# Sliding-window scores of two query heads: from zero-padded keys to two 64-row tiles of the array

## Chip, cores and metric

One core of a Trainium2 chip runs the kernel. The metric is the device time of one execution in microseconds (us); the median of three runs before the change is 1658.73 us.

## The reference, cut to what matters

One layer of a decoder is computed for a prompt of 512 tokens and for 8 samples of 4 tokens. A combined projection feeds two branches, a gated DeltaNet with 8 heads and a sliding-window attention; their sum goes through an output projection and a mixture of 64 experts. The change touches the attention over the prompt:

```
s = einsum('bnqkgd,bnskd->bnkgqs', q, k) * 64 ** -0.5     # 4 blocks of 128 queries, 256 keys each
s = where(valid, s + bias, -inf)                         # T5 bias by head and distance
m = max(max(s, -1), sink)
p = exp(s - m);  p = p / (sum(p, -1) + exp(sink - m))
o = einsum('bnkgqs,bnskd->bnqkgd', p, v)
```

There are 16 query heads of 64 channels and 2 KV heads; eight query heads share a KV head. A block of 128 queries sees its own 128 keys and the 128 before them; the first block sees its own alone.

## The kernel before, in words

The order of work is written out by hand: each engine has its own instruction list, and counting semaphores tie them. After a start-up part (norm of the input, rows of K and V, gates), every engine runs a loop over h = 0..7. Turn h computes DeltaNet head h and the two query heads 2h and 2h+1, which lie in one group of 128 channels: the channels of the first of them (u = 0) on partitions 0 to 63 of `sqT`, those of the second (u = 1) on 64 to 127. After the loop come the samples' attention, the output projection, routing and the experts.

Within a turn TensorE first projects (L1121 to L1128, then the rows of L1146 in four portions with other products between them), then builds the triangular inverses of the four 128-row chunks by repeated squaring: `square(k)` and `grow(k)` (both through the helper at L1152), six levels. ScalarE and VectorE copy each level out of PSUM (L875, L1685, L1689). The attention's four blocks n = 0..3 are laced between these levels: `scores(n)` (L1230), the softmax on VectorE (`softmax(n)`, L1701 to L1706: add the bias, maximum, maximum with the sink, negate, sink minus maximum), the exponentials on ScalarE (`probs(n)`, L882), transposes (`turn_p(n)`, L1245), a copy of them (`ptc(n)`, L891), and the product with V (`pv(n)`, L1258). Small 32-row products for the samples (L1269, L1281, L1288, L1296) stand ahead of each `scores(n)` on TensorE's queue; each waits for VectorE (`s_smp_done`). The recurrence over the chunks (L1328 to L1346) ends the turn.

`kz` holds the keys four times over: `kz[:, u, kv, :]` has the keys of KV head kv on the 64 partitions of half u and zeros on the other half. So `scores(n)` multiplies all 128 rows of `sqT` with `kz[:, u, kv]`, once for each u, and the zeros leave the other query head out. Its address depends on h through `ds(kv)`. Both results lie in one PSUM bank, bank 7 for even n, bank 5 for odd n, and one addition of VectorE over both adds the bias. GpSimd clears `kz` at the start (L630).

GpSimd's part of a turn is `gm` (L671) and a small product (L673) for the decays, two masks of the exponentials (L676, L678), the output gates and the state's stores.

Of the kernel before, what the change touches and what calls it, by code (L numbers as in the profile page):

```python
# [8 lines left out]
ALU = mybir.AluOpType  # L9
ACT = mybir.ActivationFunctionType  # L10
AX = mybir.AxisListType
P = 128
# [5 lines left out]
class Chain:  # L18
# [12 lines left out]
    def step(self, ins):  # L31
        self.inc(ins)
        self.eng.wait_ge(self.sem, self.value())
# [9 lines left out]
def ds(i, n=1):  # L43
    return bass.ds(i, n)
# [6 lines left out]
def program(nc, x_prompt, x_sample, conv_state, dn_state, cache_k, cache_v, w_in, conv_w, a_log, dt_bias, dn_norm_w,  # L51
# [4 lines left out]
    TP, TS = x_prompt.shape[0], x_sample.shape[0]  # L56
    NP = TP // P
    NT = NP + 1
# [5 lines left out]
    HD = 64  # L64
# [20 lines left out]
    with ExitStack() as ctx:  # L85
# [6 lines left out]
        PB = [ctx.enter_context(nc.psum_tensor(f"PB{i}", [P, 512], F32)) for i in range(8)]  # L92
# [14 lines left out]
        sc = sb("sc", [P, 256])  # L107
# [4 lines left out]
        def cut(*shape, parts=P):  # L112
            n = 1
            for s in shape:
                n *= s
            a = arena[0:parts, top[0]:top[0] + n]
            top[0] += n
            assert top[0] <= 37632, top[0]
            if len(shape) == 2:
                return a.rearrange("p (a b) -> p a b", a=shape[0])  # L120
            if len(shape) == 3:
                return a.rearrange("p (a b c) -> p a b c", a=shape[0], b=shape[1])
            if len(shape) == 4:
                return a.rearrange("p (a b c d) -> p a b c d", a=shape[0], b=shape[1], c=shape[2])
            return a
# [1 line left out]

        hT = cut(KC, T)
        nmix = cut(KC)
        kz = cut(2, 2, TP)  # L130
        skd = cut(2, TS)
        kvrow = cut(NT, 4 * HD)
        qz = cut(B, 2, 2, 16)
# [51 lines left out]
        Vm = sb("Vm", [TS, B, P])  # L185
        wqT = sb("wqT", [P, B, 2, L])
        wqo = sb("wqo", [P, 2, TS])
        xh = kz.rearrange("p a b c -> p (a b c)")
        biasS = sb("biasS", [P, 2, 133])
        mixer_end = top[0]  # L190

# [424 lines left out]
        def _(pool):  # L616
# [9 lines left out]
            for t in (ones[:, :], m_le[:, :], m_gt[:, :], m_ge[:, :], blk[:, :, :], bsel[:, :]):  # L626
                ch.inc(pool.memset(t, 1.0))
            ch.inc(pool.memset(ident[:, :], 0.0))
            for t in (rawP[:, :, 0:3], kz, qz.rearrange("p b v u k -> p (b v u k)"), scal, sc[:, 80:160]):
                ch.inc(pool.memset(t, 0.0))  # L630
            pool.memset(eps_t[:, 0:1], EPS).then_inc(s_setup0, 1)
            pool.memset(eps_t[:, 1:2], -0.5 * 4.852030263919617).then_inc(s_setup0, 1)
# [36 lines left out]
            with pool.Fori(0, H) as h:  # L669
                pool.wait_ge(s_hs_ready, h * 2 + 1)  # L670
                pool.tensor_tensor(gm, m_le[:, :].unsqueeze(1).to_broadcast([P, NP, P]),  # L671
                                   hsc[:, 0, 0:NP].unsqueeze(2).to_broadcast([P, NP, P]), ALU.mult).then_inc(s_gm_ready, 1)
                pool.tensor_scalar(sS[:, 8, 0:TS], s_le[:, :], hsc[0:TS, 0, NP:NT], None, ALU.mult).then_inc(s_gm_ready, 1)  # L673

                pool.wait_ge(s_E_exp, h + 1)
                pool.tensor_tensor(Es, E, m_gt[:, :].unsqueeze(1).to_broadcast([P, NP, P]), ALU.mult).then_inc(s_Em_ready, 1)  # L676
                pool.wait_ge(s_Em_ready, h * 2 + 1)
                pool.tensor_tensor(E, E, m_ge[:, :].unsqueeze(1).to_broadcast([P, NP, P]), ALU.mult).then_inc(s_Em_ready, 1)  # L678

                for i, n in enumerate(gate_rows):  # L680
                    R = rows_of[n]
                    pool.wait_ge(s_rows_done, 1 + h * NT + (i + 1))
                    pool.tensor_tensor(gates[0:R, n, 0, :], gates[0:R, n, 0, :], gates[0:R, n, 1, :], ALU.mult).then_inc(s_ss_done, 1)
                    pool.wait_ge(s_ss_done, h * NT + (i + 1))
                    pool.tensor_tensor(gates[0:R, n, 0, :], gates[0:R, n, 0, :], dnw[0:R, :], ALU.mult).then_inc(s_gate_done, 1)
                    if i == 2:
                        pool.wait_ge(s_crow_ready, h + 1)
                        pool.sem_inc(s_pool_passed, 1)
                        pool.dma_start(p_conv[:, :, ds(h * P, P)], crow[0:3, :, :]).then_inc(s_conv_out, 16)
                        pool.dma_start(s_conv[:, :, ds(h * P, P)], crow[3:27, :, :]).then_inc(s_conv_out, 16)  # L690
                pool.wait_ge(s_smp_ps, h * 11 + 8)
                pool.tensor_tensor(Sb[:, :, :], Sb[:, :, :], hgl.unsqueeze(2).to_broadcast([P, B, P]), ALU.mult).then_inc(s_decay_done, 1)
                pool.wait_ge(s_sW_done, h * 3 + 3)
                pool.tensor_tensor(Vm[:, :, :], sS[:, 6, :].unsqueeze(1).to_broadcast([TS, B, P]),
                                   bsel[:, :].unsqueeze(2).to_broadcast([TS, B, P]), ALU.mult).then_inc(s_Vm_done, 1)
                pool.wait_ge(s_S_done, h * NP + NP)
                pool.sem_inc(s_pool_passed, 1)
                pool.dma_start(p_dn[ds(h), :, :].rearrange("a k v -> (a k) v"), St).then_inc(s_pdn_out, 16)
                pool.wait_ge(s_sS_done, 1 + h + 1)
                pool.sem_inc(s_pool_passed, 1)  # L700
                pool.dma_start(s_dn.rearrange("b h k v -> h k b v")[ds(h), :, :, :].rearrange("a k b v -> (a k) b v"), Sb[:, :, :]).then_inc(s_sdn_out, 16)

                pool.wait_ge(s_conv_out, h * 32 + 32)
                pool.wait_ge(s_pdn_out, h * 16 + 16)
                pool.wait_ge(s_sdn_out, h * 16 + 16)
                pool.sem_inc(s_stored, 1)
# [62 lines left out]
        def _(act):  # L769
# [26 lines left out]
            act.activation(g8(2), g8(2), ACT.Ln).then_inc(s_g_ready, 1)  # L796
            act.wait_ge(s_kd_ps, 1)
            for v in range(2):
                act.activation(kz[v * HD:(v + 1) * HD, v, v, :], PB[4][v * HD:(v + 1) * HD, :], ACT.Copy).then_inc(s_kd_done, 1)
                act.activation(skd[v * HD:(v + 1) * HD, v, :], PB[5][v * HD:(v + 1) * HD, 0:TS], ACT.Copy).then_inc(s_kd_done, 1)  # L800
            act.wait_ge(s_ba_ready, 6)
            gs = tmp[:, 280:424]
# [251 lines left out]
        def _(pe):  # L1054
# [51 lines left out]
            with pe.Fori(0, H) as h:  # L1106
# [48 lines left out]
                qT = qk[:, 0, 0:TP].rearrange("p (n k) -> p n k", n=NP)  # L1155
                kT = qk[:, 1, 0:TP].rearrange("p (n k) -> p n k", n=NP)
                rows(0)
                pe.wait_ge(s_gm_ready, h * 2 + 2)
                pe.wait_ge(s_cst_ready, h + 1)
                for n in range(NP):  # L1160
                    last = mm(PB[7][:, n * P:(n + 1) * P], gm[:, n, :], m_gt[:, :], start=True, stop=True)
# [58 lines left out]
                def scores(n):  # L1220
                    lo = P if n == 0 else 0
                    if n == 0:
                        pe.wait_ge(s_Et_done, h + 1)
                    elif n == 1:
                        pe.wait_ge(s_rows_done, 1 + h * NT + 4)
                    else:
                        pe.wait_ge(s_sc_add, h * NP + (n - 1))
                    bank = PB[7 if n % 2 == 0 else 5]
                    for u in range(2):
                        last = mm(bank[:, u * 256 + lo:(u + 1) * 256], sqT[:, n * P:(n + 1) * P],  # L1230
                                  kz[:, u, ds(kv), (n - 1) * P + lo:(n + 1) * P].rearrange("p a k -> p (a k)"), start=True, stop=True)
                    last.then_inc(s_sc_ps, 1)

                def turn_p(n):
# [29 lines left out]
                pe.wait_ge(s_rows_done, 1 + h * NT + NT)  # L1264
                tr(b6[0:TS, 224:352], ks_, ident[:, :])
                tr(b6[0:TS, 352:480], co[:, 2, TP:T], ident[:, :]).then_inc(s_smp_ps, 1)
                pe.wait_ge(s_gm_ready, h * 2 + 2)
                pe.sem_inc(s_pe_passed, 1)
                mm(b6[0:TS, 0:TS], sS[:, 8, 0:TS], s_gt[:, :], start=True, stop=True).then_inc(s_smp_ps, 1)  # L1269
                scores(0)  # L1270
# [264 lines left out]
        def _(dve):  # L1535
# [62 lines left out]
            dve.wait_ge(s_kd_ps, 1)  # L1598
            for q in range(2):
                lo, hi = slice(32 * q, 32 * q + 32), slice(HD + 32 * q, HD + 32 * q + 32)  # L1600
                cp(kz[hi, 1, 0, :], PB[4][lo, :]).then_inc(s_kd_done, 1)
                cp(kz[lo, 0, 1, :], PB[4][hi, :]).then_inc(s_kd_done, 1)
                cp(skd[hi, 0, :], PB[5][lo, 0:TS]).then_inc(s_kd_done, 1)
                cp(skd[lo, 1, :], PB[5][hi, 0:TS]).then_inc(s_kd_done, 1)
            dve.wait_ge(s_slots_moved, 16)
            KD = 92
            with dve.Fori(0, H) as h:
                ch.loop(h, KD)

# [81 lines left out]
                def softmax(n):  # L1691
                    lo = P if n == 0 else 0
                    a = att[:, n % 2, :]
                    bank = PB[7 if n % 2 == 0 else 5]
                    if n >= 2:
                        dve.wait_ge(s_pt_ps, h * NP + (n - 1))
                        dve.wait_ge(s_p_exp, h * 3 * NP + 3 * (n - 1))
                    dve.wait_ge(s_sc_ps, h * NP + (n + 1))
                    dve.wait_ge(s_bias_in, 16)
                    snk = sinkb[:, ds(h * 2, 2)]  # L1700
                    step(tt(sm[:, n % 2, :, lo:], bank[:, :].rearrange("p (u k) -> p u k", u=2)[:, :, lo:],  # L1701
                            bias[:, ds(h * 2, 2), lo:], ALU.add))
                    step(dve.tensor_reduce(a[:, 0:2], sm[:, n % 2, :, lo:], AX.X, ALU.max))
                    step(tt(a[:, 0:2], a[:, 0:2], snk, ALU.max))
                    step(ts(a[:, 2:4], a[:, 0:2], -1.0, None, ALU.mult))
                    tt(a[:, 4:6], snk, a[:, 0:2], ALU.subtract).then_inc(s_sc_add, 1)  # L1706
# [401 lines left out]
```

## Time and profile before

| what | us |
|---|---|
| median of 3 runs | 1658.73 (1657.37 to 1659.74) |
| the profiled execution | 1663.34 |
| its span, first to last instruction | 1661.6 |
| TensorE matmul busy | 1418.0 (85%) |
| VectorE busy | 827.4 (50%) |
| ScalarE busy | 333.9 (20%) |
| GpSimd busy | 235.0 (14%) |
| L1230 (scores), TensorE busy, 128 matmul instructions | 32.8 |

PE is TensorE's matmul and PEld its weight load, DVE is VectorE, ACT ScalarE, POOL GpSimd, SP the engine that issues most DMAs; a q behind a name is the sequencer, which waits and issues. A row of the timeline reads: start, length in us, engine, line, operation, written tile, read tiles, shapes, count, and in brackets the idle time before it and what ended that. Ends of matmuls are modelled, so the modelled lengths of consecutive matmuls overlap. The granted clock is a share of TensorE's 2.4 GHz.

### The profile page before, as it was taken

Reading aid. Unit: us, or ns where it says so; the run is one execution under the profiler, and the core shown is the slowest. Engines: PE = TensorE matmul, PEld = TensorE weight load, DVE = VectorE, ACT = ScalarE, POOL = GpSimd, SP = SyncE. Lnnn points to the kernel's source line nnn. Section 1 sums busy time; section 2 is a strip of 40 time slices with the busy share of each in tenths; the row PEclk is TensorE's granted clock in tenths of the full one; section 3 lists DMA queues with packets and bytes.
Section 4 is the critical chain, followed back from the end, with each engine's and each line's share of the span. In section 5 each row is a group of like instructions: output and inputs, shape, how many; then the busy total and the mean of one; then the engine's idle time right before and its main releaser. Section 6 shows DMA issues by size and latency. Waiting matters only on the chain.

```text
span 1661.6 us, 20978 instructions
## 1 busy us (share of the span) xinstructions
PE 1418.0 (85%) x6824; PEld 811.9 (49%) x6824; DVE 827.4 (50%) x1742; ACT 333.9 (20%) x901; POOL 235.0 (14%) x356
## 2 busy tenths in 40 slices
PE   5799999999999999999999878866887878888791
PEld 4557558466485575765846754532332323233230
DVE  1386476774865857748667522462322323222225
ACT  3122123122221231222212311100111101111112
POOL 2210111021101210111012100013111111111100
PEclk9899799998998999989999879867998989899895
DMA  8821020130210302102101240169999999999985
GB/s 190 152 53 39 27 68 23 38 79 27 53 38 27 90 2 71 45 27 53 38 27 39 115 162 40 47 242 291 420 411 415 403 413 398 403 387 417 401 331 187
DMA packets 126880, 277.79 MB, mean 167 GB/s; under 512 B 21500, under 2 KB 95158, under 8 KB 102134
## 3 DMA queue, kind: packets, MB, share of 16 engines
q1 hardware_dynamic: 103990, 196.21, 33.3%
q10 hardware_dynamic: 10704, 66.06, 11.0%
q0 software_dynamic: 12160, 15.19, 2.9%
q8 instruction: 13, 0.21, 0.1%
q14 instruction: 13, 0.11, 0.0%
HBM read 272.43 MB, written 30.62 MB: 182 GB/s over the span
## 4 chain that ended last, share of the span: by engine, by line
PE 65%; DMA 21%; DVE 7%; ACT 4%; issue 2%; SPq 0%; ACTq 0%; DVEq 0%; POOLq 0%; POOL 0%
DMA arena<-in_w_up 16%; PE PB L1128 13%; PE PB L1146 10%; PE PB L1482 9%; PE PB L1152 7%; PE PB L1406 4%; DMA arena<-in_w_gate 3%; PE PB L1230 2%; PE PB L1123 2%; PE PB L1258 2%; DVE arena L1628 1%; PE PB L1121 1%; PE PB L1346 1%; PE PB L1337 1%; PE PB L1085 1%
## 5 line engine op out<-in xcount | busy, mean ns | idle before, releaser
L1482 PE MATMUL PB<-arena 128*64 128x512 f32 x1024 | 268.9, 674 | 87.2 <-DMA arena<-in_w_up 71.6
L1128 PE MATMUL PB<-arena 128*128 128x512 f32 x512 | 224.0, 595 | 0.0
L1482 PEld LDWEIGHTS PB<-arena 128*64 128x64 f32 x1024 | 77.6, 154 | 250.5 <-issue 153.4
L2000 DVE TENSOR_SCALAR arena<-arena 128x256 f32<-128x256 f32 x32 | 9.5, 296 | 340.4 <-ACT arena L993 340.2
L1152 PE MATMUL PB<-arena 128*128 128x128 f32 x1280 | 167.6, 286 | 6.2 <-ACT arena L871 5.5
L1146 PE MATMUL PB<-arena 128*128 128x384 f32 x512 | 170.8, 487 | 0.0
L1152 PEld LDWEIGHTS PB<-arena 128*128 128x128 f32 x1280 | 156.8, 199 | 14.9 <-ACT arena L871 7.4
L1128 PEld LDWEIGHTS PB<-arena 128*128 128x128 f32 x512 | 96.0, 190 | 118.6 <-issue 118.1
L932 ACT ACTIVATE arena<-PB 128x512 f32<-128x512 f32 (+3 forms) x116 | 59.9, 520 | 396.4 <-PE PB L1490 224.3
L1502 PE MATMUL PB<-arena 128*64 128x512 f32 x512 | 118.6, 605 | 11.1 <-issue 9.6
L1146 PEld LDWEIGHTS PB<-arena 128*128 128x128 f32 x512 | 95.4, 190 | 63.2 <-issue 3.8
L1628 DVE RECIPROCAL arena<-sig 128x384 f32<-128x384 f32 (+1 forms) x40 | 102.0, 2550 | 1.4
L1656 DVE RECIPROCAL arena<-arena 128x544 f32<-128x544 f32 x24 | 85.3, 3554 | 0.8
L1502 PEld LDWEIGHTS PB<-arena 128*64 128x64 f32 x512 | 35.5, 138 | 71.0 <-issue 66.1
L1406 PE MATMUL PB<-arena 128*128 128x512 f32 x128 | 58.7, 620 | 0.4 <-DVE arena L1833 0.4
L722 POOL COPY gidx<-gidx 128x1 int32 (+1 forms) x32 | 5.9, 184 | 366.1 <-PE PB L1472 258.6
L2002 DVE RECIPROCAL arena<-arena 128x256 f32<-128x256 f32 x32 | 56.1, 1753 | 1.1
L676 POOL TENSOR_TENSOR arena<-arena,m_gt 128x512 f32<-128x512 f32 x8 | 12.4, 1555 | 291.9 <-ACT arena L855 291.9
L1123 PE MATMUL PB<-arena 128*32 128x256 f32 x128 | 51.0, 586 | 0.0
L1124 PE MATMUL PB<-arena 128*32 128x256 f32 x128 | 51.0, 586 | 0.0
L875 ACT ACTIVATE arena<-PB 128x512 f32<-128x512 f32 x48 | 28.7, 597 | 107.5 <-PE PB L1152 107.5
L1689 DVE TENSOR_TENSOR arena<-PB,arena 128x512 f32<-128x512 f32 x48 | 33.0, 688 | 33.6 <-PE PB L1152 32.7
(433 smaller groups left out, 2025.6 us busy)
## 6 DMA issues: line engine op xcount, KB each, us to landing
arena<-in_w_gate SPq DMA_DIRECT2D x64, 1024.0 KB, 11.5
arena<-in_w_down SPq DMA_DIRECT2D x64, 1024.0 KB, 19.0
arena<-in_w_up ACTq DMA_DIRECT2D x60, 1024.0 KB, 14.8
arena<-in_w_in SPq DMA_DIRECT2D x58, 512.0 KB, 6.2
Sb<-in_state_dn SPq DMA_DIRECT2D x8, 512.0 KB, 4.0
out<-Sb POOLq DMA_DIRECT2D x8, 512.0 KB, 3.9
arena<-in_w_out SPq DMA_DIRECT2D x1, 4096.0 KB, 12.3
arena<-in_w_up SPq DMA_DIRECT2D x4, 1024.0 KB, 9.2
```

The source lines that it names most:

```text
L932: cpa = lambda o, i, **k: act.activation(o, i, ACT.Copy, **k)
L1123: mm(PB[6][64:96, 0:256], xs, wch[:, c, 0:4:2, :], start=first, stop=end)
L1124: last = mm(PB[6][96:128, 0:256], xs, wch[:, c, 1:4:2, :], start=first, stop=end)
L1128: last = mm(PB[g][:, :], wch[:, c, g, :], hT[:, c, 0:TP], start=c == 0, stop=c == KC - 1)
L1146: last = mm(gate_bank[(n + 1) % 2][0:R, 0:3 * P], hT[:, c, n * P:n * P + R], wrow[:, c, :, :].rearrange("p g k -> p (g k)"), start=c == 0, ...
L1152: last = mm(PB[bank][:, n * P:(n + 1) * P], lhs[:, n, :], rhs[:, n, :], start=start, stop=stop)
L1406: last = mm(PB[2 * (n % 2) + q][:, :], hT[:, c, n * P:(n + 1) * P], wo[:, c, q * 512:(q + 1) * 512], start=c == 0, stop=c == KC - 1)
L1482: last = mm(gu_bank[a][half[k], :], xT[:, a, c, half[k]], wgu[a][:, k, :, c, :], start=c == 0, stop=c == KC - 1)
L1502: last = mm(PB[4 + q][half[k], :], hidT[:, a, c, half[k]], wdn[a][:, k, c, q * 512:(q + 1) * 512], start=c == 0, stop=c == FE // P - 1)
L1628: step(dve.reciprocal(gates[0:R, n, :, :], s))
L1656: step(dve.reciprocal(ex[:, g, :], ex[:, g, :]))
L2002: dve.reciprocal(hb[:, a, :], hb[:, a, :]).then_inc(s_hid_own, 1)
```

## The change

The keys of a KV head are stored once for each half of the partitions, in `kz[:, kv, :]`, with no zeros between. At the start of each turn GpSimd copies the half of `kz` that belongs to this turn's KV head into `kcur`, so that TensorE reads a fixed address. `scores(n)` multiplies rows 0 to 63 of `sqT` with rows 0 to 63 of `kcur`, and rows 64 to 127 with rows 64 to 127: two tiles of 64 rows of the array. Their results go to two banks, 5 for u = 0 and 7 for u = 1, in the left or right half by the parity of n. Since both blocks now share the banks, every block's scores wait for the softmax of the block before (`s_sc_add`). VectorE adds the bias in two instructions, one for each bank. GpSimd no longer clears `kz`.

```
-        kz = cut(2, 2, TP)
+        kz = cut(2, TP)
+        kcur = cut(TP)
...
-            for t in (rawP[:, :, 0:3], kz, qz.rearrange("p b v u k -> p (b v u k)"), scal, sc[:, 80:160]):
+            for t in (rawP[:, :, 0:3], qz.rearrange("p b v u k -> p (b v u k)"), scal, sc[:, 80:160]):
...
                 pool.tensor_scalar(sS[:, 8, 0:TS], s_le[:, :], hsc[0:TS, 0, NP:NT], None, ALU.mult).then_inc(s_gm_ready, 1)
+                pool.wait_ge(s_o_done, 1 + h * NT)
+                pool.tensor_copy(kcur, kz[:, ds(h // 4), :].rearrange("p a k -> p (a k)")).then_inc(s_gm_ready, 1)
...
                     if n == 0:
                         pe.wait_ge(s_Et_done, h + 1)
-                    elif n == 1:
                         pe.wait_ge(s_rows_done, 1 + h * NT + 4)
+                        pe.wait_ge(s_gm_ready, h * 3 + 3)
                     else:
-                        pe.wait_ge(s_sc_add, h * NP + (n - 1))
-                    bank = PB[7 if n % 2 == 0 else 5]
+                        pe.wait_ge(s_sc_add, h * NP + n)
+                    pe.sem_inc(s_pe_passed, 1)
                     for u in range(2):
-                        last = mm(bank[:, u * 256 + lo:(u + 1) * 256], sqT[:, n * P:(n + 1) * P],
-                                  kz[:, u, ds(kv), (n - 1) * P + lo:(n + 1) * P].rearrange("p a k -> p (a k)"), start=True, stop=True)
+                        half = slice(u * HD, (u + 1) * HD)
+                        last = mm(PB[5 + 2 * u][:, (n % 2) * 256 + lo:(n % 2 + 1) * 256], sqT[half, n * P:(n + 1) * P],
+                                  kcur[half, (n - 1) * P + lo:(n + 1) * P], start=True, stop=True)
                     last.then_inc(s_sc_ps, 1)
...
-                    step(tt(sm[:, n % 2, :, lo:], bank[:, :].rearrange("p (u k) -> p u k", u=2)[:, :, lo:],
-                            bias[:, ds(h * 2, 2), lo:], ALU.add))
+                    for u in range(2):
+                        ch.inc(tt(sm[:, n % 2, u, lo:], PB[5 + 2 * u][:, (n % 2) * 256 + lo:(n % 2 + 1) * 256],
+                                  bias[:, ds(h * 2 + u), lo:].rearrange("p a k -> p (a k)"), ALU.add))
+                    dve.wait_ge(s_dve_own, ch.value())
```

## Rows read from the trace of the kernel before

**Rows 1.** The page, the chain that ended last, shares by engine
```profile
PE 65%; DMA 21%; DVE 7%; ACT 4%; issue 2%; SPq 0%; ACTq 0%; DVEq 0%; POOLq 0%; POOL 0%
```

**Rows 2.** The chain in order of time: start, us, what; first projections of three heads
```profile
76.30 7.06 PE PB L1128 x16
...
191.45 7.06 PE PB L1128 x16
...
300.65 7.06 PE PB L1128 x16
```

**Rows 3.** The chain in order of time, scores in the fourth head, blocks 0 and 2
```profile
471.40 0.64 PE PB L1230 x4
...
480.00 1.12 PE PB L1230 x4
```

**Rows 4.** Timeline, TensorE, block 2 of the fourth head and what follows
```profile
480.00 1.13 PE L1230 MATMUL PB<-arena 128*128 x4
...
480.96 0.55 PE L1258 MATMUL PB<-arena,pT 128*128 x4
```

**Rows 5.** One line, L1230: ns min/median/max; matmuls of block 2, sequencer in all heads
```profile
L1230 PE MATMUL PB<-arena x4: 379/379/479, 480.0 to 480.7; 128*128 x4
...
L1230 PEldq FUSED_REGOPS  x48: 46/51/128, 137.4 to 919.8; - x48
```

**Rows 6.** Timeline, TensorE, start of the fourth head, four 32-column tiles
```profile
403.36 0.53 PE L1121 MATMUL PB<-arena 128*32 128x192 f32 x1
...
403.38 0.64 PE L1124 MATMUL PB<-arena 128*32 128x256 f32 x1
...
403.68 0.53 PE L1121 MATMUL PB<-arena 128*32 128x192 f32 x1
```

**Rows 7.** Timeline, TensorE, a 64-row stage between two whole-array ones
```profile
416.85 0.34 PE L1135 MATMUL PB<-ident,srow 64*128 64x64 f32 x2
...
417.12 0.70 PE L1128 MATMUL PB<-arena 128*128 128x512 f32 x1
```

**Rows 8.** Timeline, VectorE around block 0, and TensorE's load of L1281
```profile
471.30 0.68 DVE L1685 COPY arena<-PB 128x512 f32<-128x512 f32 x1
...
471.90 0.33 DVE L1718 TENSOR_SCALAR sS<-PB,hbeta 32x128 f32<-32x128 f32 x1
...
472.88 0.40 DVE L1701 TENSOR_TENSOR sm<-PB,arena 128x256 f32<-128x256 f32 x1
...
475.35 0.18 DVE L1730 TENSOR_TENSOR sS<-PB,sS 32x32 f32<-32x32 f32 x1
...
475.64 0.09 PEld L1281 LDWEIGHTS PB<-ident,sS 32*32 32x32 f32 x1 [0.22 <-issue]
```

**Rows 9.** Groups by line and shape: count, busy us, mean ns, idle before
```profile
L2004 DVE TENSOR_TENSOR arena<-arena,PB 128x256 f32<-128x256 f32 x32 | 13.5, 420 | 1.1
...
L1629 DVE TENSOR_TENSOR arena<-arena,PB 128x128 f32<-128x128 f32 x32 | 9.2, 287 | 1.1
```

**Rows 10.** Timeline, VectorE in blocks 1 and 2, scores of block 3
```profile
477.08 0.69 DVE L1701 TENSOR_TENSOR sm<-PB,arena 128x512 f32<-128x512 f32 x1 [0.74 <-PE PB L1230]
...
483.00 0.16 DVE L1706 TENSOR_TENSOR att<-arena,att 128x2 f32<-128x2 f32 x1
...
484.74 1.13 PE L1230 MATMUL PB<-arena 128*128 x4
```

**Rows 11.** Timeline, GpSimd and ScalarE at the start, GpSimd in the fourth head
```profile
2.97 2.54 POOL L630 MEMSET arena<- 128x9 f32 x4
...
10.46 1.06 ACT L779 ACTIVATE arena<-mixed 128x1024 f32<-128x1024 f32 x1 [8.27 <-DMA arena<-in_norm_mix_w]
...
407.82 1.04 POOL L671 TENSOR_TENSOR arena<-m_le,arena 128x512 f32<-128x512 f32 x1 [3.41 <-DMA out<-Sb]
```

**Rows 12.** Stretches: busy us of PE, PEld, DVE, ACT, POOL; granted clock; DMA share, GB/s
```profile
163.40:190.70 27.30, 25.30 (x127) 17.50 (x127) 10.78 (x39) 4.44 (x21) 6.41 (x6) 0.50 0.09 25
...
497.90:501.30 3.40, 3.40 (x16) 2.75 (x14) 2.10 (x9) 0.15 (x1) 0.82 (x1) 0.50 0.00 0
501.30:511.60 10.30, 8.21 (x42) 5.26 (x40) 4.64 (x15) 4.04 (x20) 2.51 (x2) 1.00 0.02 6
```

More of the change, by code:

```diff
@@ L187, in program @@
         wqo = sb("wqo", [P, 2, TS])
-        xh = kz.rearrange("p a b c -> p (a b c)")
         biasS = sb("biasS", [P, 2, 133])
@@ L798, in _ @@
             for v in range(2):
-                act.activation(kz[v * HD:(v + 1) * HD, v, v, :], PB[4][v * HD:(v + 1) * HD, :], ACT.Copy).then_inc(s_kd_done, 1)
+                act.activation(kz[v * HD:(v + 1) * HD, v, :], PB[4][v * HD:(v + 1) * HD, :], ACT.Copy).then_inc(s_kd_done, 1)
                 act.activation(skd[v * HD:(v + 1) * HD, v, :], PB[5][v * HD:(v + 1) * HD, 0:TS], ACT.Copy).then_inc(s_kd_done, 1)
@@ L1157, in _ @@
                 rows(0)
-                pe.wait_ge(s_gm_ready, h * 2 + 2)
+                pe.wait_ge(s_gm_ready, h * 3 + 2)
                 pe.wait_ge(s_cst_ready, h + 1)
@@ L1266, in _ @@
                 tr(b6[0:TS, 352:480], co[:, 2, TP:T], ident[:, :]).then_inc(s_smp_ps, 1)
-                pe.wait_ge(s_gm_ready, h * 2 + 2)
+                pe.wait_ge(s_gm_ready, h * 3 + 2)
                 pe.sem_inc(s_pe_passed, 1)
@@ L1600, in _ @@
                 lo, hi = slice(32 * q, 32 * q + 32), slice(HD + 32 * q, HD + 32 * q + 32)
-                cp(kz[hi, 1, 0, :], PB[4][lo, :]).then_inc(s_kd_done, 1)
-                cp(kz[lo, 0, 1, :], PB[4][hi, :]).then_inc(s_kd_done, 1)
+                cp(kz[hi, 0, :], PB[4][lo, :]).then_inc(s_kd_done, 1)
+                cp(kz[lo, 1, :], PB[4][hi, :]).then_inc(s_kd_done, 1)
                 cp(skd[hi, 0, :], PB[5][lo, 0:TS]).then_inc(s_kd_done, 1)
@@ L1605, in _ @@
             dve.wait_ge(s_slots_moved, 16)
-            KD = 92
+            KD = 96
             with dve.Fori(0, H) as h:
@@ L1693, in softmax @@
                     a = att[:, n % 2, :]
-                    bank = PB[7 if n % 2 == 0 else 5]
                     if n >= 2:
```

## The prediction

> **What bounds the kernel now.** I began with the chain of waits by engine: TensorE holds 65% of it, DMA 21%, VectorE 7% [rows 1]. In its list in order of time the first projection of a head (L1128) shows how long a head lasts: 115.15 us for the first (76.30 to 191.45) and 109.20 for the second (191.45 to 300.65); the six later ones repeat that closely [rows 2]. So some 880 of the 1661.6 us are eight heads, bound by TensorE; the rest, mostly experts whose weights arrive by DMA, the change does not touch. Inside a head the same list has the four score blocks of L1230 on the chain: 0.64 us for block 0 and 1.12 for block 2, which stands for three alike [rows 3].
>
> The timeline then says what block 2 consists of: four matmul instructions (two query heads, each in two passes), the first at 480.00, and the next line's first at 480.96, so a block takes 0.96 [rows 4]. Its first matmul lasts 479 ns against 379 for the others [rows 5]: a weight load of 0.10 that nothing hides, as a 32-row stage stands ahead. So a pass takes (0.96 - 0.10)/4 = 0.215.
>
> **The change part by part.** *Scores as two 64-row tiles.* The trace has no pair of row tiles that work at once. The nearest rows are the four 32-column tiles of L1121 to L1124: their first passes start within 0.02 us of each other (403.36 to 403.38), the second pass of L1121 only at 403.68 [rows 6]. Four different tiles ran at once, pass by pass. For two row tiles I take the same: 2 x 0.215 = 0.43 of streaming in place of 0.86. The other end is no overlap at all, 0.86.
>
> What comes after a block gets dearer. Now L1230 and what follows use the whole array. After the change a 64-row stage stands between, and the trace has one: the two 64-row transposes of L1135 between two runs of L1128. They start at 416.85 and their modelled end is 417.19; the next whole-array matmul starts at 417.12, thus 0.07 before that end [rows 7]. For a score pass, whose modelled end lies 0.379 after its start, that is a gap of 0.379 - 0.07 - 0.215 = 0.09 after the last pass; and then the first load of the new stage is exposed, 0.10 as in rows 5. The way in costs what it costs now, since a 32-row stage (L1269, L1281, L1288, L1296) stands ahead of each block already. New block: 0.10 + 0.43 + 0.09 + 0.10 = 0.72, against 0.96: 0.24 saved. Without any overlap it is 1.15, 0.19 lost.
>
> A rule of the Trainium skill speaks against the change here: "TensorEngine Tiling (Array Packing)", Tiling Modes, Key Properties, says that a change of tiling mode, other than a change of tile, drains TensorE. Rows 7 agree, with the 0.09 above. With the rule the sum is the one below; without it each block would save 0.43 and the total would come to 9.1 us.
>
> *Block 0 gains nothing.* The squaring that follows it needs VectorE's copy of L1685, which runs from 471.30 to 471.98; the block itself lies between 471.40 and 472.04 on the chain [rows 3, 8]. A shorter block waits for that copy.
>
> *The split bias addition on VectorE (L1701).* One instruction over both heads becomes two, since they lie in two banks. For blocks 1 to 3, 128x512 at 0.69 becomes two of 128x256; L2004, of that form and out of PSUM, lasts 0.420. For block 0, 0.40 becomes two of 128x128, and L1629 of that form lasts 0.287 [rows 8 to 10]. Instructions in a row overlap (L1718 starts 0.08 before L1685 ends [rows 8]), so I get 2 x 0.42 - 0.08 - 0.69 = +0.07 and 2 x 0.287 - 0.08 - 0.40 = +0.09, and take 0.10 for block 0, with a register instruction more. In block 0 this is on the path: the VectorE rows from L1685 at 471.30 to L1730 at 475.35 show no idle time, and PE's L1281 waited for L1730 (it ends at 475.53, the load comes at 475.64 after 0.22 idle) [rows 8]. So 0.10 is lost per head; bounds 0, were the pair as fast as the one, and 0.17 with no overlap. In blocks 1 to 3 VectorE waits for the scores before L1701, 0.74 us in block 1 [rows 10]; it gets them some 0.3 earlier, which covers 0.07. If that cover went, 0.21 per head.
>
> *Semaphores.* Scores of block n now wait for the softmax of block n-1, in every block. Ahead of blocks 1 and 2 stands a matmul that waits for a later VectorE instruction anyway. Block 3 is the new one: the last step it waits for ends at 483.16, the block starts at 484.74 [rows 10], so there is 1.6 us of slack; behind the wait on TensorE's queue stand the products with V, the transposes and the next squaring, for which ScalarE and VectorE wait. The added semaphore instruction ahead of each block is priced by the register instruction that vanishes (48 of them, median 51 ns [rows 5]): nothing for blocks 2 and 3, 0.05 for block 1, whose wait now stands alone ahead of the load; bounds 0 and 4 x 0.05.
>
> *Copy of the keys on GpSimd.* 128x512 per head. The product L671 of that size lasts 1.04 and starts at 407.82 [rows 11]; the copy stands behind it and ahead of the wait for the exponentials, some 60 us before scores are due (471.40). The wait for the head before is over by then, since GpSimd has just waited for that head's state stores. Bounds 0 and 8 x 1.04; I take nothing. *Clearing of kz.* At the start it falls away, up to 2.54 us of GpSimd; but ScalarE's first work waits for the input's DMA until 10.46 [rows 11], later than all of that. Nothing.
>
> **Sum.** Per head 3 x 0.24 - 0.10 - 0.05 = 0.57; times eight, 4.6 us. The ends: all overlap and no drain or extra cost, 3 x 0.43 = 1.29 per head, 10.3; no overlap with 0.17 and 0.20 lost, -(3 x 0.19 + 0.37) = -0.94 per head, 7.5 us slower. The profiled execution took 1663.34 (span 1661.6 and 1.7 around it), so it would take 1658.7; the median of the runs is 1658.73, 4.6 under that execution, and the same subtraction gives 1654.1, which I forecast.
>
> **Rivals.** *1. The two tiles do not run side by side (slower).* For it: no row shows two row tiles at once. Against: rows 6 show four column tiles doing so. Price: 3 x 0.19 + 0.15 = 0.72 per head, 5.8 us, 1664.5. It decides once the streaming of a block exceeds 0.62 (0.43 plus the 0.19 that drain and load take back).
>
> *2. Half an overlap; the change does only half of what it says.* If the second head's first pass begins only when the first head's second pass has begun, three passes stand in a row: 0.10 + 0.645 + 0.19 = 0.94, about as now. With 0.15 lost against 3 x 0.02 the change costs 0.1 per head, 1659.4: no change. The interleaved starts of rows 6 speak against it. The Trainium skill, "TensorE: Matmul & The Clock Gate", Part 3, says that matmuls start strictly in program order, and by that rule one head's two passes would come ahead of the other's; rows 6 do not look like that.
>
> *3. The clock after a head.* In the first head TensorE's clock is at 1.2 GHz (granted 0.50) from 163.40 to 190.70. In a later head it falls too, but 497.90 to 501.30 is low and then it is back at 2.4 GHz (1.00 until 511.60) [rows 12]. To that I put down the 5.95 us between the first head and the others. Heads last as long as this pattern takes to repeat, so each later head meets it at the same point of its work. With heads 0.57 shorter the point wanders, and which kind a head becomes may change in either direction. If the first head recovers early too: 4.6 + 5.95 = 10.5, 1648.2. If one more head stays low: 1.4 slower, 1660.1, no change; two more, 7.3 slower, 1666.0. The rows show both kinds and don't say where one turns into the other.
>
> *4. Gain on paper only.* The scores come earlier, but ScalarE's probabilities or VectorE bind the next step. Blocks 1 to 3 have TensorE on the chain, so I see at most half lost: 1656.4.
>
> **How the numbers follow.** A difference of 0.2% (3.3 us) is about what can be told from no change. Chances: forecast 0.36 (its own range 1652 to 1657; 0.29 faster, 0.07 within); early recovery 0.15; one head more at the low clock 0.09; two or more 0.15; no overlap 0.10; half 0.09; gain on paper 0.06 (0.02 faster). Faster 0.46, same 0.29, slower 0.25. The range runs from 1645, past the early recovery, to 1666, where two more low heads end; left out are more than two such heads, the far end of no overlap, and several early ones.
>
> **What would show it.** Right: L1230's matmuls of the two heads start within 0.02 us of each other; from a block's first matmul to the next line's first 0.72 instead of 0.96 in blocks 1 to 3; the load after it exposed; block 0 no shorter on the chain and L1281 0.1 later; heads of 108.6. The forecast is wrong if passes start one behind the other, if a block still takes 0.9 or more, or if heads differ from each other by some 6 us, which would be the clock.

## The result and the profile after

The changed kernel takes 1646.94 us (median of 6 runs, 1640.67 to 1649.11) against 1659.24 for the kernel before on the same chip (1657.24 to 1667.30): 12.3 us faster, ratio 0.9904 with a 95% interval of 0.9875 to 0.9933. The forecast was 4.6 us. The profiled execution took 1647.58 (span 1645.9), 15.8 under that of before.

First the page's line on the chain of waits by engine, against [rows 1]:

```profile
PE 64%; DMA 22%; DVE 7%; ACT 4%; issue 2%; SPq 1%; ACTq 0%; DVEq 0%; POOLq 0%; POOL 0%
```

Then the chain in order of time, the first projections of all eight heads (L1130, the L1128 of before), against [rows 2]:

```profile
77.43 7.06 PE PB L1130 x16
...
186.78 7.06 PE PB L1130 x16
...
293.86 7.06 PE PB L1130 x16
...
402.00 7.06 PE PB L1130 x16
...
509.08 7.06 PE PB L1130 x16
...
614.74 7.07 PE PB L1130 x16
...
722.87 7.07 PE PB L1130 x16
...
831.63 7.06 PE PB L1130 x16
```

The bound is the same. But heads are no longer alike: 109.35, 107.08, 108.14 and 107.08 us for the first four, then 105.66, 108.13 and 108.76. The seven together take 831.63 - 77.43 = 754.2, where before they took 115.15 + 6 x 109.20 = 770.4. So 16.2 us came out of seven heads: 5.8 out of the first and 10.4 out of the six behind it. The first head starts 1.1 later than before, at the end of a weight transfer ahead of the loop; the traces below begin theirs between 75.98 and 77.39 with no pattern by kernel.

Next the timeline of TensorE in the fourth head, against [rows 4, 5]: first of the stretch from 468.10 to 468.14 alone, below the line of dots block 1 and block 2 with what follows each:

```profile
468.13 0.49 PE L1233 MATMUL PB<-arena 64*128 64x256 f32 x2
...
468.13 0.70 PE L1233 MATMUL PB<-arena 64*128 64x256 f32 x4
468.76 0.44 PE L1248 MATMUL PB<-ident,sm 128*128 128x128 f32 x2
...
471.99 0.70 PE L1233 MATMUL PB<-arena 64*128 64x256 f32 x4
472.75 0.65 PE L1261 MATMUL PB<-arena,pT 128*128 x4
473.24 0.60 PE L1248 MATMUL PB<-ident,sm 128*128 128x128 f32 x4
```

Within that short stretch the first passes of both heads have started. The four rows of a block last 0.70 together, where they lasted 1.13.

Then the chain around block 0, against [rows 8]:

```profile
462.92 0.60 DVE arena L1685
463.52 0.61 DVE arena L1688
464.14 0.14 issue
464.27 0.79 PE PB L1154 x5
```

VectorE's two additions of block 0, in the timeline:

```profile
465.02 0.47 DVE L1704 TENSOR_TENSOR sm<-PB,arena 128x128 f32<-128x128 f32 x2
465.53 0.42 DVE L1707 TENSOR_REDUCE att<-sm 128x2 f32<-128x256 f32 x1
```

And the stretches by granted clock: the end of the first head, which answers to [rows 12], and the fifth head from its middle on (columns as there):

```profile
165.40:175.60 10.20, 9.67 (x39) 7.79 (x37) 3.63 (x15) 1.47 (x5) 2.32 (x2) 0.50 0.01 2
175.70:182.40 6.70, 5.12 (x41) 3.12 (x44) 4.49 (x14) 2.97 (x16) 1.38 (x2) 1.00 0.03 10
182.50:185.90 3.40, 3.40 (x40) 2.34 (x34) 1.89 (x10) 0.00 (x0) 0.07 (x1) 0.50 0.53 154
571.60:575.00 3.40, 3.40 (x20) 3.17 (x19) 1.97 (x11) 1.54 (x6) 0.00 (x0) 0.50 0.00 0
575.00:614.60 39.60, 36.38 (x309) 29.84 (x307) 24.13 (x81) 12.07 (x46) 5.34 (x4) 1.00 0.05 15
```

Before, the first head was low for 27.3 us without a break; now it recovers in between. The fifth head, which was low twice for 10.2 us in all, is low once, for 3.4, and keeps the full clock to its end. That is the shortest head, 105.66.

How much of the 16.2 us is work and how much clock? Up to the last small product ahead of the products of the carried state (L1304 before, L1307 after) the second head runs at the full clock in both traces; it comes 79.97 us after the head's first projection before, 79.49 after. So the edits save 0.48 us a head by themselves, 3.4 in seven heads and 3.9 in eight. The other 12.8 would be the clock. That is an inference from two traces; the experiments test it.

### The profile page after: what moved, and what is told of

Read it like the earlier page. It is cut to its first block, busy times and chain, and to the rows that moved or that the text cites. A ratio compares the mean times of both kernels' runs of the same rounds, so it can differ in the third digit from the quotient of the medians.

```text
span 1645.9 us, 21025 instructions
## 1 busy us (share of the span) xinstructions
PE 1396.2 (85%) x6824; PEld 794.9 (48%) x6824; DVE 830.6 (50%) x1774; ACT 333.9 (20%) x901; POOL 237.8 (14%) x363
## 4 chain that ended last, share of the span: by engine, by line
PE 64%; DMA 22%; DVE 7%; ACT 4%; issue 2%; SPq 1%; ACTq 0%; DVEq 0%; POOLq 0%; POOL 0%
DMA arena<-in_w_up 17%; PE PB L1130 14%; PE PB L1148 10%; PE PB L1485 9%; PE PB L1154 7%; PE PB L1409 4%; DMA arena<-in_w_gate 3%; PE PB L1261 2%; PE PB L1125 2%; DVE arena L1631 1%; PE PB L1123 1%; PE PB L1340 1%; PE PB L1087 1%; PE PB L1174 1%; PE PB L1233 1%
## 5 line engine op out<-in xcount | busy, mean ns | idle before, releaser
L1485 PE MATMUL PB<-arena 128*64 128x512 f32 x1024 | 263.9, 663 | 84.0 <-DMA arena<-in_w_up 69.7
L1130 PE MATMUL PB<-arena 128*128 128x512 f32 x512 | 224.0, 595 | 0.0
L1130 PEld LDWEIGHTS PB<-arena 128*128 128x128 f32 x512 | 96.0, 190 | 118.6 <-issue 118.1
L1505 PE MATMUL PB<-arena 128*64 128x512 f32 x512 | 119.5, 609 | 16.2 <-issue 13.9
L1475 PEld LDWEIGHTS PB<-ident,arena 128*128 128x128 f32 x256 | 31.8, 196 | 31.0 <-issue 31.0
L1125 PE MATMUL PB<-arena 128*32 128x256 f32 x128 | 44.2, 522 | 0.0
```

What stands on the lines that cost most here:

```text
L1125: mm(PB[6][64:96, 0:256], xs, wch[:, c, 0:4:2, :], start=first, stop=end)
L1130: last = mm(PB[g][:, :], wch[:, c, g, :], hT[:, c, 0:TP], start=c == 0, stop=c == KC - 1)
L1485: last = mm(gu_bank[a][half[k], :], xT[:, a, c, half[k]], wgu[a][:, k, :, c, :], start=c == 0, stop=c == KC - 1)
L1505: last = mm(PB[4 + q][half[k], :], hidT[:, a, c, half[k]], wdn[a][:, k, c, q * 512:(q + 1) * 512], start=c == 0, stop=c == FE // P - 1)
```

## The experiments

Theory 1: the edits save some 0.5 us a head, and the rest is what the granted clock does when the work lies differently under it. Theory 2: the operations of the change are worth the whole 1.5 us a head. In the sections below "direct" is the shift of that same product (L1304 or its counterpart) at the full clock, per head; totals are ratios to the kernel before in the same session.

### Other changes of a head's length, with and without the row tiles

**b_short**, the kernel before with less work in the scores: in blocks 2 and 3 it leaves out the second query head's scores against one half of its keys.

```
-                        last = mm(bank[:, u * 256 + lo:(u + 1) * 256], ...
+                        hi = P if u == 1 and n >= 2 else 0
+                        last = mm(bank[:, u * 256 + lo:(u + 1) * 256 - hi], ...
```

> The kernel before, without row tiles, fixed keys or the split addition; in the scores of blocks 2 and 3 the second query head's matmul takes 128 of its 256 keys, so those scores are left out. Each of the two matmuls falls from some 0.43 us to 0.21, so TensorE's path in a head is 0.43 us shorter, about what the change took directly (0.48). Theory 1 (direct saving 0.5 us a head, the rest of the 12.3 us is what TensorE's granted clock does once a head is no longer 109.2 us long): the total falls by clearly more than 8 x 0.43 = 3.4 us, to 1643 to 1652 from some 1659, head lengths unequal, and the stretches at a granted clock of 0.50 move from head to head as in the changed kernel. Theory 2 (the whole 12.3 us comes from the changed operations themselves, 1.5 us a head): 1655.8, every head 108.8 us.

Ratio 0.9907 (0.9872 to 0.9941), 15 us, at a direct saving of 0.33 (79.65 against 79.98 in the first head), 2.6 us in all. Its chain:

```profile
76.55 7.06 PE PB L1128 x16
...
186.16 7.06 PE PB L1128 x16
...
292.04 7.06 PE PB L1128 x16
...
397.93 7.06 PE PB L1128 x16
```

Heads of 105.9 in place of 109.2: with no row tile, no copy of keys and no split addition, the kernel gets all that the change got. Theory 2 (1655.8, heads of 108.8) is out. The direct part was 0.1 smaller than I expected.

**a_long**, the changed kernel with its saving given back in block 3:

```
-                    for u in range(2):
+                    for u in (0, 1, 0, 1) if n == 3 else (0, 1):
```

> The changed kernel with block 3's pair of score matmuls issued twice, +0.4 us a head on TensorE's path, the result unchanged. Theory 1: the head's phase against the granted clock's falls is set anew, so the total moves by another amount than 8 x 0.43 = 3.4 us; most of the 12.3 us can be lost, 1650 to 1660. Theory 2: the row tiles and the fixed keys are all there, so 1647 + 3.4 = 1650.4, every head 0.43 us longer than in the changed kernel.

Ratio 0.9949 (0.9925 to 0.9973; 1652.26), so nearly half the gain went with 0.43 us a head. The direct saving left is 0.04 (79.92 against 79.97), 0.3 us in all, and still 8 us are gained: its first five heads alternate between 108.6 and 106.5. The two theories' ranges both held this; but a kernel whose work is less by 0.04 us a head and that is 8 us faster cannot owe that to its work.

**b_long** and **b_long2**, the kernel before with the second query head's scores issued twice in block 3, and in blocks 2 and 3:

```
-                    for u in range(2):
+                    for u in (0, 1, 1) if n == 3 else (0, 1):     # b_long; n >= 2 in b_long2
```

> The kernel before with the second query head's score matmul of block 3 issued twice, +0.43 us a head on TensorE's path, the result unchanged. Theory 1 (direct part plus whatever the granted clock's pattern does at the new head length): the total does not follow the added 3.4 us; heads come out unequal or locked to another pattern, anywhere from 1650 to 1668, and a total at or below that of the kernel before would show that shortening is not what brought the extra gain. Rival (the time follows the work, 8 x 0.43 us): 1660 + 3.4 = 1663.8, every head 109.64 us with the same three low stretches.

> The same in blocks 2 and 3, +0.86 us a head. Theory 1: again not on a line with the added work (6.9 us); 1652 to 1672. Rival: 1667.2, every head 110.07 us.

Ratios 1.0065 (1.0037 to 1.0092), 11 us, and 1.0194 (1.0161 to 1.0227), 32 us, for direct costs of 0.43 and 0.87 a head, 3.5 and 6.9 us in all. My hope that a longer head might do as well as a shorter one failed: more work cost more, three and nearly five times over. Both kernels took longer than theory 1 allowed (1670.41 against at most 1668, 1691.18 against at most 1672), and longer than the rival's 1663.8 and 1667.2. So the time does not follow the added work alone, as theory 1 says, but I had sized the clock's part too small here too. In b_long2 what only the first head had before [rows 12] befalls three heads in a row. The stretch that is low in the second head:

```profile
274.30:301.40 27.10, 25.10 (x125) 17.30 (x126) 10.73 (x38) 4.43 (x21) 6.31 (x6) 0.50 0.08 23
```

And on its chain the first projections of the fourth and fifth head:

```profile
418.22 7.06 PE PB L1128 x16
...
534.24 7.06 PE PB L1128 x16
```

116.0 us for the fourth head, 6.8 more than before; the second and third take as long.

### The same pair with the clock held up

If the clock makes the difference, it must shrink to the direct part when the clock no longer falls. **b_warm** and **a_warm** are the two kernels with matmuls whose results nobody reads, put where TensorE waits; the banks they write are free by then.

```
+                def warm(bank, lo, cols, count):
+                    for _ in range(count):
+                        mm(PB[bank][:, lo:lo + cols], ident[:, :], hT[:, 0, 0:cols], start=True, stop=True)
...
                 square(1)
+                pe.wait_ge(s_Et_done, h + 1)
+                warm(7, 0, 256, 3)
                 pe.wait_ge(s_rows_done, 1 + h * NT + NT)
...
                 each(3, Rk, Tt).then_inc(s_wT_ps, 1)
+                pe.wait_ge(s_sc_add, h * NP + NP)
...
                     if n:
+                        warm(5, 0, P, 1)
                         pe.wait_ge(s_S_done, h * NP + n)
...
+                    warm(5, 0, HD if n else P, 1 if n else 3)
                     pe.wait_ge(s_vn_done, h * NP + (n + 1))
...
+                warm(0, 0, 256, 3)     # behind the last matmul of the turn
```

> The kernel before with matmuls whose results nobody reads put into TensorE's waits: three of 256 columns before the wait for the fourth gate rows, three of 128 before the first wait of the recurrence, one of 64 or 128 before each later one, three of 256 after the last matmul of a head. Theory 1: the granted clock stays at 1.00 through the loop, a head takes some 106 us instead of 109.2, total 1659 - 25 = 1634 (1628 to 1645). Theory 2: the clock may rise too, but says nothing about the change. If the extra matmuls end late, a head gets longer by up to 1 us and the total may not fall.

> The changed kernel with the same extra matmuls in the same waits. Theory 1: with the clock at 1.00 in both, this pair differs by the direct part alone, 8 x 0.48 = 3.9 us (3 to 5), so some 1630, heads of 105.5 us; the changed kernel's advantage of 12.3 us shrinks to a third. Theory 2: the pair differs by about 12 us, as without the extra matmuls.

Ratios 0.9894 (0.9866 to 0.9922) and 0.9855 (0.9820 to 0.9889). The gap between the two narrowed from 0.0096 to 0.0039, about 6 us, more than the 3.9 of theory 1; the medians (1643.99 and 1633.62) lie 10.4 apart, hardly less than the 12.3 of the plain pair. So the totals decide nothing here, and the clock was not held: it still falls some 87 us into each of the first seven heads of b_warm and five of a_warm's, whose other two take 105.0 with no low stretch. Heads with the same low time differ by about the direct part: with 3.4 us low 106.9 to 107.1 against 106.2 to 106.6, with 6.8 low 108.28 against 107.79.

What stands ahead of that fall is the same in all traces: eight products of the carried state whose moving operand has 8 columns (L1313 before, L1316 after). **b_full** and **a_full** widen it to 64 columns, of which 8 are used. The weight loads set the pace there, so it costs little. The products go to bank 5, and the later extra matmuls to bank 7:

```
-        wqT = sb("wqT", [P, B, 2, L])
+        wqT = sb("wqT", [P, 2 * B, 2, L])     # upper half cleared once
...
+                pe.wait_ge(s_sc_add, h * NP + NP)
...
-                    last = mm(b6[:, b * 2 * L:(b + 1) * 2 * L], Sb[:, b, :], wqT[:, b, :, :]...
+                    last = mm(PB[5][:, b * 64:(b + 1) * 64], Sb[:, b, :], wqT[:, b:b + 8, :, :]...
```

> b_warm with one more edit: the eight products of the carried state with 8 columns each, before the recurrence (the stretch right ahead of the last fall of the granted clock that b_warm still shows, 87 us into a head), take 64 columns each, of which 8 are used. Theory 1: the granted clock stays at 1.00 for whole heads, all of 105.6 us (105.0 for a_warm's two heads without a low stretch, plus 0.5 to 0.6), total 1636 to 1640. Theory 2 says nothing about this kernel alone.

> a_warm with the same wider products. Theory 1: heads of 105.0 us at a granted clock of 1.00, and the pair differs by the direct part alone, 0.5 to 0.6 us a head, 4 to 5 us in all: 1631 to 1635, and the scatter from run to run is smaller than in the changed kernel (1640.7 to 1649.1). Theory 2: the pair differs by 12 us. If the products of 64 columns are not hidden beside their weight loads, both heads are up to 0.5 us longer.

1632.40 (ratio 0.9845, 0.9818 to 0.9872) and 1625.66 (0.9811, 0.9783 to 0.9838). The stretch from the second head to the eighth in b_full (the clock is the third figure from the end):

```profile
182.00:815.10 633.10, 616.76 (x3350) 418.69 (x3348) 448.58 (x930) 167.78 (x486) 94.69 (x120) 1.00 0.17 46
```

The same in a_full:

```profile
181.50:811.90 630.40, 611.48 (x3350) 409.33 (x3348) 453.32 (x954) 167.65 (x486) 97.41 (x126) 1.00 0.17 46
```

The first projections of the second and the eighth head on b_full's chain:

```profile
182.08 7.06 PE PB L1128 x16
...
815.22 7.06 PE PB L1128 x16
```

And on a_full's:

```profile
181.60 7.06 PE PB L1130 x16
...
812.00 7.06 PE PB L1130 x16
```

Six heads take 633.14 and 630.40: 105.52 and 105.07 each. At one clock the change is worth 0.45 us a head, 3.6 in eight, close to the 0.48 of the first reading. Both totals lie below the expected ranges (1636 to 1640 and 1631 to 1635), and the medians differ by 6.7, where I expected 4 to 5. In the two traces the loops differ by 3.7; the other 2.3 lie behind the loop, nearly all in the experts, which are the same code in both. I did not find their cause.

This also prices the clock. In the kernel before, a later head was low twice; here is the fifth, with the stretch between:

```profile
607.10:610.50 3.40, 3.40 (x16) 2.75 (x14) 2.11 (x9) 0.16 (x1) 0.83 (x1) 0.50 0.00 0
610.50:620.80 10.30, 8.22 (x42) 5.26 (x40) 4.64 (x15) 4.03 (x20) 2.52 (x2) 1.00 0.02 6
620.80:627.60 6.80, 6.28 (x63) 4.40 (x65) 3.53 (x15) 0.24 (x1) 2.33 (x3) 0.50 0.30 86
```

Such a head took 109.20, and 105.52 at 2.4 GHz, so its 10.2 us at 1.2 GHz cost 3.7. Over seven heads the clock cost 770.4 - 7 x 105.52 = 31.8 us before and 754.2 - 7 x 105.07 = 18.7 after. Of the 16.2 us, 13.1 are clock and 3.1 work. This takes the extra matmuls and the wider products to add nothing to a head. Up to the products of the carried state they don't: these start 85.06 us into a head in the kernel before, in b_warm and in b_full alike. Behind that point no run separates them.

**b_full_long2** puts b_long2's edit into b_full, to see whether the extra matmuls multiply anything by themselves:

> b_full (extra matmuls in the waits and the wider products, clock at 1.00 through the heads) with the second query head's score matmul issued twice in blocks 2 and 3, the edit that made the kernel before 32 us slower. Theory 1 (an edit of the scores has a direct part, and the clock's falls multiply it): here only the direct part is left, about 0.43 us a block on TensorE's path where no other wait hides it: heads of 105.9 to 106.4 us in place of 105.52 and 3 to 7 us in all, 1635 to 1639. Rival (the added matmuls cost 32 us by themselves, by delaying VectorE or the recurrence): heads of 109 us, some 1660.

1640.89, ratio 0.9882 (0.9858 to 0.9906), 6 us over b_full by the ratios and 8.5 by the medians, a little above the expected 1635 to 1639. Two of its starts:

```profile
182.36 7.06 PE PB L1128 x16
...
288.75 7.06 PE PB L1128 x16
```

Heads of 106.39, 0.87 longer: with the clock held, a head grows by its added work and by nothing else. The edit that costs 32 us under a falling clock costs 6 to 8.5 under a steady one.

**a_wide** is the changed kernel with the wider products alone:

> The changed kernel with only the eight products of the carried state at 64 columns in place of 8, no extra matmuls. Theory 1: the low stretch 87.7 us into a head goes, those at 62.7 and 101 us stay in part; heads of 105 to 107 us, total 1636 to 1645. Rival (the products have nothing to do with the falls): 1647 with the same falls at 87.7 us.

1639.01, ratio 0.9877 (0.9851 to 0.9903). Its runs lie within 3.7 us of each other, those of the changed kernel within 8.4. Five of its first seven heads take 106.1, the other two 108.4; two starts on its chain:

```profile
184.85 7.06 PE PB L1130 x16
...
290.92 7.06 PE PB L1130 x16
```

As expected the fall at 87.7 us is gone from every head, and those at 63 and 101 stay in part. The products take 1.95 us in place of 1.90 (L1324 of a_full against L1316 of the changed kernel). One fall is removed by columns that hold nothing of use.

### Is it the row groups that overlap?

**a_onehalf** puts both matmuls on the same 64 rows of the array:

```
-                        half = slice(u * HD, (u + 1) * HD)
+                        half = slice(0, HD)
```

> The changed kernel with both score matmuls on partitions 0 to 63, so one row group of the array for both; the second query head's scores are left out (the first's stand in their place). If the gain of a block is the overlap of two row groups, the second matmul's passes start behind the first's, some 0.43 us later, and a block takes 1.0 to 1.1 us in place of 0.63 to 0.75, a head at equal granted clock 0.43 us a block longer for the blocks on TensorE's path. If it is the 64 rows or the two banks instead, the passes still start 7 ns apart and the block stays at 0.63 to 0.75 us. The total is one draw of the clock's pattern and tells nothing by itself.

Block 2 of its second head and what follows, in the timeline:

```profile
263.55 1.13 PE L1233 MATMUL PB<-arena 64*128 64x256 f32 x4
264.61 0.55 PE L1261 MATMUL PB<-arena,pT 128*128 x3
```

A block takes 1.06 to the next line's first matmul, 0.10 more than the whole-array block before and 0.3 more than the tiles on two row groups. So the overlap needs two row groups; 64 rows or two banks alone give nothing. Up to L1307 its second head is 0.64 us longer than before (80.61 against 79.97), and its one run took 1672.55, between b_long and b_long2, as its direct cost is. A kernel without GpSimd's copy of the keys (a_nocopy) gave no time, so no run shows what the copy and the fixed address are worth by themselves.

## Why the prediction was right in kind and wrong in size

- *Two tiles at once: right.* Both heads' first passes start within the stretch of 0.04 us shown. The tiles run pass by pass, as the column tiles of [rows 6] did. Rivals 1 and 2 are out: the second head's first pass starts ahead of the first head's second (block 2: 471.987, 471.994, then 472.307, 472.314). The rows don't name the tile, but on one row group two passes never start so close: a_onehalf's four of block 2 start at 263.552, 263.873, 264.088 and 264.304. The Trainium skill's rule that matmuls start strictly in program order ("TensorE: Matmul & The Clock Gate", Part 3) is not borne out for the passes of two tiles.
- *Price of the change of mode: right.* In block 3 the last pass starts at 476.957 and the next line at 477.26; less 0.215 of streaming that is a gap of 0.09, as read off [rows 7], where the drain that the Trainium skill states ("TensorEngine Tiling (Array Packing)", Tiling Modes, Key Properties) stood beside it. The exposed load shows behind block 2: L1261 to L1248 takes 0.49 where L1258 to L1245 took 0.39.
- *Net saving of a block: near.* From a block's first matmul to the next line's first the trace has 0.63, 0.77 and 0.63 for blocks 1 to 3 of the fourth head, where I had 0.72. Part of the cost shows only behind that point: from the start of one small product to the next, block 1 gave 0.16, block 2 0.16, block 3 0.23, against 0.19, 0.24 and 0.24. Block 1 starts 0.11 later behind its small product, not 0.05; block 2 has 0.06 of issue ahead of L1261, which I did not see coming.
- *Block 0 gains nothing: right.* The squaring still waits for VectorE's copy (463.52 to 464.13), the block being over by then.
- *Split addition: right, slightly dear.* The pair takes 0.47 (forecast 0.49), and L1284 comes 0.07 later; I took 0.10.
- *Copy of the keys: right.* It runs at 401.66 for 0.60, 62 us ahead of the scores.
- *Sum: 0.48 a head, forecast 0.57.* By the pair at a steady clock 0.45, 3.6 us for eight heads. So far the forecast of 4.6 stands.
- *The step that failed is what the sum left out and rival 3 sized.* The sum kept the clock's pattern of every head as it was, which puts the clock's part at nothing; the runs showed it to be the larger part, 13.1 of the 16.2 us in seven heads. Rival 3 saw that shorter heads move against it, but it took the later heads' pattern for the good state, with only the first head's 5.95 us to win and each change in a later head a loss. They were not in the good state: b_full's 105.52 shows 3.7 us of clock in each 109.20. That was to be had from the trace: a later head is low for 3.4 us from 497.90 [rows 12] and again for 6.8 after 511.60, where that row ends. Adding up the low time, 27.3 + 6 x 10.2 = 88.5 us in seven heads, and losing at most half of it, gives a stake of up to 44 us (31.8 by b_full) instead of 5.95. I gave the favourable side 0.15 and sized it 10.5; the result was 12.3, by that side. The first head gave 5.8, what rival 3 had for it; the 10.4 from the six later heads are what it did not see. That the total landed so near to rival 3's 10.5 is therefore partly luck.
- *What stays open.* Which heads fall, for how long, and why 0.04 us less (a_long) already frees 8 us while 0.43 more costs 11, no run explains. Nor does a run show rival 3's ground for the wandering, that a head lasts as long as the clock's pattern takes to repeat. The traces are one execution each; executions of one kernel spread by up to 19 us, those with the steady clock by 6 or 7. And the 2 us of the steady pair behind the loop have no cause that I can show.

The version that beats both kernels is a_full, 1625.66 us, 1.9% under the kernel before: most of that is the steady clock, and 3.6 us in the heads are the row tiles with their copy and split addition.

## What to carry to other kernels

Where a loop on TensorE dips to the lower granted clock in every turn, first hold the clock up and measure the loop then: that gives each edit's own worth, and the low time is likely the larger prize. Before costing an edit there, add up the low time of all turns and put it into the range on both sides, since an edit of 0.4 us a turn moved the total by 11 to 15 us in either direction. Two 64-row tiles do run side by side, but around them some 0.2 us of drain and exposed load come off each use, so only a long enough stream pays.

## What the runs showed that I had not expected

- 0.87 us more work a head cost 32 us in all, 6.9 of it work; 0.33 less gave 15, 2.6 of it work.
- Eight products with 64 columns in place of 8 take 1.95 us in place of 1.90, and with them no head falls to 1.2 GHz 87 us after its start.
- With the extra matmuls in the waits and the wider products together the clock stayed at 1.00 for 633 us, and the heads of one trace agreed within 0.06 us. The extra matmuls alone did not do it.
